# The value product of a hybrid layer in five items of 512 columns, its weights loaded in two halves of the contraction

## The chip, the core and the metric

The kernel runs on one core of one Trainium2 chip. The core has five engines with a queue each: TensorE (PE, with its weight loads as PEld), VectorE (DVE), ScalarE (ACT), GpSimd (POOL) and SyncE (SP, which here only issues DMAs). They meet at semaphores. The metric is the device time of one execution in microseconds; it is given as the median of a few runs. Data is in fp32; a product is split in a high and a rest part of the reduced type fp32r and done in three matmuls (high by high, high by rest, rest by high).

## What is computed

One layer with three token mixers and a mixture of experts for 512 prompt tokens and 64 sample tokens (576 in all, D_MODEL = 1024). Only the first step matters here: the norm, and the columns 1024 to 1535 of one wide projection, which are the values v of the attention.

```python
def token_mixers(u, lp, past):
    B, T, _ = u.shape
    proj = u @ lp['w_in']                       # w_in: 1024 x 4104
    q, k, v, xb, gb, zc, xbc, dtr = jnp.split(proj, IN_SPLITS, axis=-1)
...
    u = rmsnorm(h, lp['g_mix'])
    # v: (576, 512) = u (576, 1024) @ w_in[:, 1024:1536]
```

All else (keys, queries, convolutions, scan, gates, output, routing, experts) follows behind and is the same in both kernels.

## The kernel before, in words

**Tiles.** The 576 rows are five row tiles t = 0 to 4 (128 rows, the last 64). Each goes through four steps. `x_norm(t)`: ACT squares and sums the tile in `x0`, DVE and ACT make the inverse root, DVE scales the tile. `x_turn(t)`: TensorE transposes it in eight steps into PSUM (`za` or `zb`), DVE multiplies by the gain `gains_mix` into `u_rest`. `u_split(t)`: ACT copies it to `u_high_r` (fp32r), DVE subtracts to `u_rest_r`. The gain itself is loaded by ACT's queue, turned by TensorE (`gain_turn`) and copied by ACT (`gain_up`).

**Value weights.** w_in[:, 1024:1536] has 1024 rows (the contraction, eight blocks k of 128) by 512 columns: 2 MB in `v_raw`. SP loads it behind row tiles 0 and 1 as two halves of 256 columns, all k, in runs of 1 KB (L651), ahead of row tiles 2 to 4. `v_split(j)`, j = 0 to 3, takes one column half and four k: ACT copies to `v_high` (L1320), DVE subtracts to `v_rest` (L1725). Semaphores `high_r` and `rest_r` count these and the later splits.

**Items.** `ITEMS` lists the projection's pieces in order. Item n takes a PSUM bank of `pj` and is evicted by ACT (for v: L1363, into `v_sb`). TensorE's item n waits until item n-2 is evicted. The value product is items 0 to 9: (column half 0, tiles 0 and 1), (half 1, tiles 0 and 1), then for tiles 2, 3 and 4 half 0 and half 1. An item is 8 k by three matmuls (L791 to L793) with 256 moving columns. Behind them come the items of the keys (288 columns, two per weight unit), and so on.

**Jobs.** What has to be done ahead of item n stands in `JOBS[n]`, and each engine goes through the same list: the jobs of n in the order in which they were added, then item n. The splits of weight units were added first: unit u is split `AHEAD` = 3 items before its first use. Then x_turn(t), u_split(t) and x_norm(t+1) for t = 2, 3, 4. Steps before item 0 are written out at the end of each engine's program. The key units 1 and 2 are loaded into `first`, whose place is free from the start; SP issues the loads of the following units into the ring, where the value weights lie, when the last value item is done (L684). GpSimd writes masks and issues small parameter DMAs; it waits for the second half of the value weights, then issues the load of `w_dt` (L2391) and five parameter rows (L2395), which the step `params` ahead of the first key item needs.

Of the kernel before, what the change touches and what calls it, by code (L numbers as in the profile page):

```python
# [27 lines left out]
P = 128  # L28
# [78 lines left out]
ITEMS = [("v", c, t, 0, 0) for ts in ((0, 1), (2,), (3,), (4,)) for c in range(2) for t in ts]  # L107
# [35 lines left out]
NVP = 4  # L143
FIRST_SLOT = 2 * NSLOT
# [51 lines left out]
for _t in range(2, NT):  # L196
    job(2 * _t - 1, "x_turn", _t)
    job(2 * _t - 1, "u_split", _t)
    if _t + 1 < NT:
        job(2 * _t - 1, "x_norm", _t + 1)  # L200
job(2 * NT, "params", 0)
# [82 lines left out]
def trunk_and_experts(nc, a, o):  # L284

    ctx = ExitStack()
    with ctx:
# [293 lines left out]
        def last_bank(k):  # L581
# [6 lines left out]
            route_ps route_in routed mix_high mix_rest vp_in consts gmix_in ut_u ut_h high_r rest_r wdt_r  # L588
# [51 lines left out]
        def _(sp):  # L640
# [5 lines left out]
            for t, (o0, n) in enumerate(TT):  # L646
                src = a["x_prompt"][0, o0:o0 + n, :] if t < NT - 1 else a["x_sample"][0]
                sp.dma_start(x0[0:n, t, :], src).then_inc(x_in[t], 16)
                if t == 1:
                    for c in range(2):  # L650
                        sp.dma_start(v_raw[:, :, 256 * c:256 * (c + 1)],  # L651
                                     a["w_in"][0, :, 1024 + 256 * c:1280 + 256 * c].rearrange("(k p) n -> p k n", p=P)
                                     ).then_inc(unit_in[3 * c], 16)
# [109 lines left out]
        def _(pe):  # L763
# [31 lines left out]
            def item(n):  # L795
# [8 lines left out]
                if u in SPLIT_NO:  # L804

                    pe.wait_ge(S["rest_r"], SPLIT_NO[u + 1 if kind in "zo" else u] + 1)
                elif u is not None and kind != "v":
                    pe.wait_ge(unit_in[s], 16 * ARRIVAL[u])
# [24 lines left out]
                elif kind == "v":  # L833
                    o0, rows_n = TT[hh]
                    half = slice(256 * c, 256 * (c + 1))
                    for k in range(KD):
                        if hh == 0 and k % 4 == 0:
                            pe.wait_ge(S["rest_r"], 2 * c + k // 4 + 1)
                        uh, ur = (x[:, k, o0:o0 + rows_n] for x in (u_high_r, u_rest_r))
                        m = product(bank[0:rows_n, 0:256], (uh, ur), (v_high[:, k, half], v_rest[:, k, half]), k)  # L840
# [101 lines left out]
            def att_values(u):  # L942
                kind, hp, kb = ATT[u]
                w = att_a[u % 2]
                if u == 0:
                    wait_drained(pe, IDX[("v", 1, NT - 1)])
# [301 lines left out]
            def over_tables():  # L1248

                pe.wait_ge(S["route_in"], NT + 4)  # L1250
                for q, cols in enumerate((over_col, over_weight)):
                    for c in range(2 * NT):
# [6 lines left out]
                                             state_out, ffn_turn, logits, ranks, table, weights, params, x_turn)}  # L1259
            x_turn(0)  # L1260
            gain_turn()
# [35 lines left out]
        def _(act):  # L1297
# [53 lines left out]
            def item(n):  # L1351
# [9 lines left out]
                elif kind == "v":  # L1361
                    r = TT[hh][1]
                    m = act.activation(v_sb[0:r, hh, 256 * c:256 * (c + 1)], bank[0:r, 0:256], ACT.Copy)  # L1363
# [42 lines left out]
                if n == IDX[("v", 1, NT - 1)]:  # L1406
# [277 lines left out]
        def _(dve):  # L1684
# [37 lines left out]
            def v_split(j):  # L1722
                ks, half = slice(4 * (j % 2), 4 * (j % 2) + 4), slice(256 * (j // 2), 256 * (j // 2) + 256)
                dve.wait_ge(S["high_r"], j + 1)
                dve.tensor_tensor(v_rest[:, ks, half], v_raw[:, ks, half], v_high[:, ks, half], ALU.subtract  # L1725
# [579 lines left out]
            x_turn(0)  # L2305
            u_split(0)
            v_split(0)
            x_turn(1)
            v_split(1)
            u_split(1)  # L2310
            v_split(2)
            v_split(3)
            x_norm(2)
# [35 lines left out]
        def _(pool):  # L2349
# [39 lines left out]

            pool.wait_ge(unit_in[3], 16)  # L2390
# [228 lines left out]
```

## Time and profile before

| | |
|---|---|
| runs | 1221.39, 1208.87, 1216.23 us; median 1216.23 |
| profiled execution | span 1216.1 us |
| busy | PE 1119.0 us (92%), DVE 531.6 (44%), ACT 381.9 (31%), POOL 214.3 (18%) |
| chain that ended last | PE 56%, DMA 27%, DVE 8%, ACT 5% |

The span is the time from the first to the last instruction of one execution; busy time is the sum of an engine's instructions in it. The chain that ended last is followed back from the last instruction to what released it. The two slices that concern the change are the first ones of the 40 (30.4 us each), in which PE is busy for 4 and 9 tenths.

### The profile page before, as it was taken

To read this page: it belongs to the slowest core of one execution; us is meant where nothing else is said; L and a number is where in the kernel's file an instruction comes from. 1 tells how busy PE (TensorE), PEld (TensorE's weight loads), DVE (VectorE), ACT (ScalarE), POOL (GpSimd) and SP (SyncE) were. 2 spreads that over 40 slices of the span, in tenths; PEclk is the share of its full clock that TensorE was granted. 3 is DMA by queue.
4 is the path that set the end of the run, shared out by engine and by line. 5 is a ranking of instruction groups with operands and counts; after the bars stand their busy time and mean duration, and the time that the engine had idled before them with its cause. 6 is when DMAs were issued, how large, how long until landed. Compare 5 with 4: busy or idle time off the path is not lost.

```text
span 1216.1 us, 17158 instructions
## 1 busy us (share of the span) xinstructions
PE 1119.0 (92%) x6833; PEld 799.3 (66%) x6833; DVE 531.6 (44%) x992; ACT 381.9 (31%) x601; POOL 214.3 (18%) x230
## 2 busy tenths in 40 slices
PE   4999989899999999999999869999999999999994
PEld 4899877677988899999999853344333434333332
DVE  4331667764246465543534641333332323333336
ACT  3313666667556444433421101111110101111103
POOL 4000321332413346542310010000000000000000
PEclk9999999999999999999999959999999999999998
DMA  9279643463322212225362199999999999999982
GB/s 180 76 130 112 46 51 38 53 51 39 61 66 70 69 54 71 61 82 152 87 216 106 70 366 413 398 413 429 427 427 428 427 428 427 428 428 426 427 343 79
DMA packets 94316, 263.16 MB, mean 216 GB/s; under 512 B 5020, under 2 KB 75896, under 8 KB 81960
## 3 DMA queue, kind: packets, MB, share of 16 engines
q1 hardware_dynamic: 87664, 250.36, 61.2%
q0 software_dynamic: 3456, 6.58, 1.5%
q10 hardware_dynamic: 3128, 5.29, 1.2%
q8 instruction: 46, 0.75, 0.3%
q14 instruction: 22, 0.18, 0.0%
HBM read 258.24 MB, written 7.64 MB: 219 GB/s over the span
## 4 chain that ended last, share of the span: by engine, by line
PE 56%; DMA 27%; DVE 8%; ACT 5%; issue 3%; SPq 1%; ACTq 0%; DVEq 0%; POOLq 0%
DMA arena<-in_w_expert_up 22%; PE za L1164 12%; PE pj L791 10%; PE pj L793 9%; PE pj L792 9%; DMA ring<-in_w_in 3%; PE pj L818 2%; PE zb L1178 2%; DVE arena L1891 1%; DVE arena L1852 1%; DVE arena L1853 1%; DVE ring_r L1731 1%; PE zb L928 1%; ACT arena L1442 1%; ACT arena L1438 1%
## 5 line engine op out<-in xcount | busy, mean ns | idle before, releaser
L1164 PE MATMUL za<-arena 128*64 128x512 f32 x1024 | 231.9, 606 | 25.8 <-DMA arena<-in_w_expert_up 24.0
L791 PE MATMUL pj<-u_high_r,ring_r 128*128 128x288 f32 x736 | 224.1, 304 | 0.4 <-ACT arena L1360 0.4
L792 PE MATMUL pj<-u_rest_r,ring_r 128*128 128x288 f32 x736 | 216.7, 294 | 0.0
L793 PE MATMUL pj<-u_high_r,ring_r 128*128 128x288 f32 x736 | 216.7, 294 | 0.0
L1164 PEld LDWEIGHTS za<-arena 128*64 128x64 f32 x1024 | 73.1, 139 | 175.8 <-issue 138.6
L791 PEld LDWEIGHTS pj<-u_high_r,ring_r 128*128 128x128 f32 x736 | 138.2, 188 | 14.1 <-issue 11.6
L792 PEld LDWEIGHTS pj<-u_rest_r,ring_r 128*128 128x128 f32 x736 | 138.2, 188 | 0.6
L793 PEld LDWEIGHTS pj<-u_high_r,ring_r 128*128 128x128 f32 x736 | 138.0, 188 | 0.0
L1731 DVE TENSOR_TENSOR ring_r<-ring,ring_r 128x1024 fp32r<-128x1024 f32 x62 | 77.7, 1258 | 105.9 <-ACT ring_r L1325 105.9
L1178 PE MATMUL zb<-arena 128*64 128x512 f32 x512 | 113.6, 595 | 3.9 <-DMA arena<-in_w_expert_down 1.5
L1178 PEld LDWEIGHTS zb<-arena 128*64 128x64 f32 x512 | 36.2, 137 | 74.3 <-issue 71.5
L1325 ACT ACTIVATE ring_r<-ring 128x1024 fp32r<-128x1024 f32 x62 | 64.6, 1051 | 21.6 <-DMA ring<-in_w_in 16.7
L2570 POOL COPY arena<-arena 128x1 int32 (+1 forms) x15 | 2.7, 182 | 380.2 <-PE ms L1156 380.2
L2269 DVE SCALAR_TENSOR_TENSOR y_rest<-zb,arena,y_high 128x512 fp32r<-128x512 f32 x32 | 24.0, 751 | 89.0 <-ACT y_high L1607 89.0
L2253 DVE SCALAR_TENSOR_TENSOR arena<-arena,za 128x512 f32<-128x512 f32 x16 | 11.0, 687 | 117.9 <-PE za L1164 117.9
L1607 ACT ACTIVATE y_high<-zb,arena 128x512 fp32r<-128x512 f32 x32 | 22.0, 687 | 127.5 <-PE zb L1178 127.5
L791 PE MATMUL pj<-ring_r,u_high_r 128*128 128x256 f32 (+1 forms) x160 | 48.3, 302 | 12.5 <-ACT arena L1363 6.2
L1404 ACT ACTIVATE arena<-pj,arena 128x288 f32<-128x288 f32 x48 | 24.0, 500 | 106.4 <-PE pj L793 106.3
L2225 DVE TENSOR_TENSOR arena<-arena,pj 128x512 f32<-128x512 f32 (+1 forms) x90 | 57.2, 674 | 0.0
L1588 ACT ACTIVATE arena<-oa 128x512 f32<-128x512 f32 x16 | 9.6, 600 | 149.2 <-PE ms L1156 149.2
L2247 DVE SCALAR_TENSOR_TENSOR arena<-arena,za 128x512 f32<-128x512 f32 x16 | 11.0, 688 | 101.6 <-ACT arena L1591 101.6
L1591 ACT ACTIVATE arena<-za 128x512 f32<-128x512 f32 x16 | 9.6, 598 | 146.1 <-PE za L1164 146.1
(451 smaller groups left out, 2127.7 us busy)
## 6 DMA issues: line engine op xcount, KB each, us to landing
arena<-in_w_expert_gate SPq DMA_DIRECT2D x32, 2048.0 KB, 25.5
arena<-in_w_expert_up SPq DMA_DIRECT2D x32, 2048.0 KB, 17.7
arena<-in_w_expert_down SPq DMA_DIRECT2D x32, 2048.0 KB, 16.8
ring<-in_w_in SPq DMA_DIRECT2D x26, 512.0 KB, 8.7
ring<-in_w_gate SPq DMA_DIRECT2D x24, 512.0 KB, 4.3
arena<-in_x_prompt SPq DMA_DIRECT2D x8, 512.0 KB, 9.2
ring<-in_w_branch_out SPq DMA_DIRECT2D x8, 512.0 KB, 3.4
ring<-in_w_in SPq DMA_DIRECT2D x2, 1024.0 KB, 16.0
```

Source lines behind the costliest of these rows:

```text
L791: pe.matmul(out, left[0], right[0], start=k == 0, stop=False)
L792: pe.matmul(out, left[0], right[1], start=False, stop=False)
L793: return pe.matmul(out, left[1], right[0], start=False, stop=k == last - 1)
L818: m = pe.matmul(bank[:, 0:HALF], ring4[s][:, k, m_cols], oAT[:, k, cols], start=k == 0, stop=k == WT - 1)
L1164: m = pe.matmul(za[j * BLK:(j + 1) * BLK, b, :], xT[spare][:, k, j * BLK:(j + 1) * BLK], w[:, j * KD + k, :], start=k == 0, stop=k == KD - 1)
L1178: m = pe.matmul(zb[j * BLK:(j + 1) * BLK, q, :], hidT[:, k, j * BLK:(j + 1) * BLK], w[:, j * (DE // P) + k, q * 512:(q + 1) * 512], start= ...
L1325: act.activation(high_r[s], raw[s], ACT.Copy).then_inc(S["high_r"], 1)
L1404: m = act.activation(gsb[k % 2], bank[:, 0:HALF], ACT.Tanh, scale=0.5, bias=cpar[:, j:j + 1])
L1607: act.activation(y_high[:, half], zb[:, q, :], ACT.Copy, scale=weight_now).then_inc(S["yh_r"], 1)
L1731: dve.tensor_tensor(rest_r[s], raw[s], high_r[s], ALU.subtract).then_inc(S["rest_r"], 1)
L2225: dve.tensor_tensor(v, v, add_bank(k)[0:n, :], ALU.add).then_inc(S["sc_r"], 1)
L2269: dve.scalar_tensor_tensor(out=y_rest[:, half], in0=zb[:, q, :], scalar=weight_now, in1=y_high[:, half], op0=ALU.mult, op1=ALU.subtract).t ...
```

## The change

```diff
-ITEMS = [("v", c, t, 0, 0) for ts in ((0, 1), (2,), (3,), (4,)) for c in range(2) for t in ts]
+ITEMS = [("v", 0, t, 0, 0) for t in range(NT)]
...
+NVD = 2
...
 for _t in range(2, NT):
-    job(2 * _t - 1, "x_turn", _t)
-    job(2 * _t - 1, "u_split", _t)
+    job(_t - 1, "x_turn", _t)
+    job(_t - 1, "u_split", _t)
     if _t + 1 < NT:
-        job(2 * _t - 1, "x_norm", _t + 1)
-job(2 * NT, "params", 0)
+        job(_t - 1, "x_norm", _t + 1)
+job(NT, "params", 0)
...
# SyncE
                     for c in range(2):
-                        sp.dma_start(v_raw[:, :, 256 * c:256 * (c + 1)],
-                                     a["w_in"][0, :, 1024 + 256 * c:1280 + 256 * c].rearrange("(k p) n -> p k n", p=P)
+                        sp.dma_start(v_raw[:, 4 * c:4 * c + 4, :],
+                                     a["w_in"][0, 512 * c:512 * (c + 1), 1024:1536].rearrange("(k p) n -> p k n", p=P)
                                      ).then_inc(unit_in[3 * c], 16)
...
# TensorE, item of kind v
-                    half = slice(256 * c, 256 * (c + 1))
                     for k in range(KD):
-                        if hh == 0 and k % 4 == 0:
-                            pe.wait_ge(S["rest_r"], 2 * c + k // 4 + 1)
+                        if hh == 0 and k % 2 == 0:
+                            j = k // 2
+                            pe.wait_ge(*((S["rest_r"], j + 1) if j < NVD else (S["v_rest_p"], j - NVD + 1)))
                         uh, ur = (x[:, k, o0:o0 + rows_n] for x in (u_high_r, u_rest_r))
-                        m = product(bank[0:rows_n, 0:256], (uh, ur), (v_high[:, k, half], v_rest[:, k, half]), k)
+                        m = product(bank[0:rows_n, :], (uh, ur), (v_high[:, k, :], v_rest[:, k, :]), k)
...
+            pe.wait_ge(S["consts"], 1)
+            gain_turn()
             x_turn(0)
-            gain_turn()
             x_turn(1)
...
# ScalarE (and DVE likewise, with the subtraction)
             def v_split(j):
-                ks, half = slice(4 * (j % 2), 4 * (j % 2) + 4), slice(256 * (j // 2), 256 * (j // 2) + 256)
+                ks = slice(2 * j, 2 * j + 2)
                 act.wait_ge(unit_in[3 * (j // 2)], 16)
-                act.activation(v_high[:, ks, half], v_raw[:, ks, half], ACT.Copy).then_inc(S["high_r"], 1)
+                act.activation(v_high[:, ks, :], v_raw[:, ks, :], ACT.Copy).then_inc(S["high_r"], 1)
...
+            gain_up()
             x_norm(0)
             x_norm(1)
-            gain_up()
+            v_split(0)
             u_split(0)
-            v_split(0)
             v_split(1)
-            u_split(1)
             v_split(2)
             v_split(3)
             x_norm(2)
+            u_split(1)
...
# GpSimd
+            for j in range(NVD, NVP):
+                ks = slice(2 * j, 2 * j + 2)
+                pool.wait_ge(S["high_r"], j + 1)
+                pool.tensor_tensor(v_rest[:, ks, :], v_raw[:, ks, :], v_high[:, ks, :], ALU.subtract
+                                   ).then_inc(S["v_rest_p"], 1)
             pool.wait_ge(unit_in[3], 16)
```

In words: the value product becomes five items, one per row tile, with 512 moving columns. Its weights come as rows 0 to 511 and rows 512 to 1023, each in runs of 2 KB. The four splits take two k each, of all columns; ACT still makes all four high parts, DVE the rest parts of chunks 0 and 1, GpSimd those of chunks 2 and 3. TensorE waits for the chunks one by one in item 0 alone. The evictions of v are 512 wide. The waits of later items for `rest_r` are two lower, since DVE makes two fewer value splits. The gain's turn and copy come first. The jobs of the row tiles move with the items: x_turn(t) stands ahead of item t-1; before, it stood ahead of item 2t-1, the second half item of the tile before.

VectorE, from its turn of row tile 0 on, before (L1710 is the turn, L1719 the rest of u, L1725 the rest of a value chunk, L1696 to L1700 the norm):

```order
L1710 TENSOR_TENSOR u_rest<-za,gains_mix 128x4x128 x2
L1719 TENSOR_TENSOR u_rest_r<-u_rest,u_high_r 128x8x128
L1725 TENSOR_TENSOR ring_r<-ring,ring_r 128x4x256
L1710 TENSOR_TENSOR u_rest<-zb,gains_mix 128x4x128 x2
L1725 TENSOR_TENSOR ring_r<-ring,ring_r 128x4x256
L1719 TENSOR_TENSOR u_rest_r<-u_rest,u_high_r 128x8x128
L1725 TENSOR_TENSOR ring_r<-ring,ring_r 128x4x256 x2
L1696 TENSOR_SCALAR arena<-arena 128x1
L1699 RECIPROCAL arena<-arena 128x1
L1700 TENSOR_SCALAR arena<-arena 128x1024
L1710 TENSOR_TENSOR u_rest<-za,gains_mix 128x4x128 x2
L1719 TENSOR_TENSOR u_rest_r<-u_rest,u_high_r 128x8x128
```

and after (the same functions, two lines further down):

```order
L1712 TENSOR_TENSOR u_rest<-za,gains_mix 128x4x128 x2
L1727 TENSOR_TENSOR ring_r<-ring,ring_r 128x1024
L1721 TENSOR_TENSOR u_rest_r<-u_rest,u_high_r 128x8x128
L1727 TENSOR_TENSOR ring_r<-ring,ring_r 128x1024
L1712 TENSOR_TENSOR u_rest<-zb,gains_mix 128x4x128 x2
L1698 TENSOR_SCALAR arena<-arena 128x1
L1701 RECIPROCAL arena<-arena 128x1
L1702 TENSOR_SCALAR arena<-arena 128x1024
L1721 TENSOR_TENSOR u_rest_r<-u_rest,u_high_r 128x8x128
L1712 TENSOR_TENSOR u_rest<-za,gains_mix 128x4x128 x2
L1721 TENSOR_TENSOR u_rest_r<-u_rest,u_high_r 128x8x128
L1698 TENSOR_SCALAR arena<-arena 128x1
```

The two later value splits are gone from DVE, the first one stands ahead of the rest of u, and the norm of tile 2 ahead of the rest of u of tile 1.

VectorE a little further on, before, from the norm of tile 4 (64 rows) to the split of the second key unit (L1731):

```order
L1710 TENSOR_TENSOR u_rest<-zb,gains_mix 128x4x128 x2
L1719 TENSOR_TENSOR u_rest_r<-u_rest,u_high_r 128x8x128
L1696 TENSOR_SCALAR arena<-arena 64x1
L1699 RECIPROCAL arena<-arena 64x1
L1700 TENSOR_SCALAR arena<-arena 64x1024
L1731 TENSOR_TENSOR first_r<-first,first_r 128x1024
L1710 TENSOR_TENSOR u_rest<-za,gains_mix 128x4x64 x2
L1719 TENSOR_TENSOR u_rest_r<-u_rest,u_high_r 128x8x64
L1731 TENSOR_TENSOR first_r<-first,first_r 128x1024
```

and after, from the norm of tile 3:

```order
L1698 TENSOR_SCALAR arena<-arena 128x1
L1701 RECIPROCAL arena<-arena 128x1
L1702 TENSOR_SCALAR arena<-arena 128x1024
L1733 TENSOR_TENSOR first_r<-first,first_r 128x1024
L1712 TENSOR_TENSOR u_rest<-zb,gains_mix 128x4x128 x2
L1721 TENSOR_TENSOR u_rest_r<-u_rest,u_high_r 128x8x128
L1698 TENSOR_SCALAR arena<-arena 64x1
L1701 RECIPROCAL arena<-arena 64x1
L1702 TENSOR_SCALAR arena<-arena 64x1024
L1712 TENSOR_TENSOR u_rest<-za,gains_mix 128x4x64 x2
L1721 TENSOR_TENSOR u_rest_r<-u_rest,u_high_r 128x8x64
L1733 TENSOR_TENSOR first_r<-first,first_r 128x1024
```

The split of the first key unit, which stood behind the norm of tile 4, now stands ahead of the turn of tile 3 (`zb`), its split and that norm. ACT has the same order.

GpSimd, before, behind its masks:

```order
L2383 MEMSET arena 128x584
L2384 MEMSET arena 128x584
L2387 IOTA arena 128x32
L2388 IOTA arena 128x5
L2391 DMA arena<-in_w_in 128x8x8
L2395 DMA arena<-in_ssm_dt_bias 128x8
L2395 DMA arena<-in_ssm_a_log 128x8
L2395 DMA arena<-in_ssm_d 128x8
```

and after:

```order
L2383 MEMSET arena 128x584
L2384 MEMSET arena 128x584
L2387 IOTA arena 128x32
L2388 IOTA arena 128x5
L2393 TENSOR_TENSOR ring_r<-ring,ring_r 128x1024 x2
L2396 DMA arena<-in_w_in 128x8x8
L2400 DMA arena<-in_ssm_dt_bias 128x8
L2400 DMA arena<-in_ssm_a_log 128x8
L2400 DMA arena<-in_ssm_d 128x8
```

Two passes over value chunks now stand ahead of the load of `w_dt` and the parameter rows.

## Rows read from the trace of the kernel before

**Rows 1.** Windows by stage: stretch, length, busy us (count) of each engine, granted clock, DMA share, GB/s.

```profile
0.00:60.50 60.50, 40.73 (x287) 38.90 (x288) 23.46 (x36) 21.91 (x39) 15.40 (x36) 0.94 0.57 129
...
60.00:70.00 10.00, 10.00 (x78) 10.00 (x77) 2.68 (x9) 1.96 (x6) 0.00 (x0) 1.00 0.90 204
...
725.00:1216.00 491.00, 446.15 (x2040) 184.54 (x2036) 169.80 (x294) 59.57 (x106) 17.83 (x29) 0.98 0.94 397
```

**Rows 2.** TensorE's waits, 0 to 320 us: total us, times, longest.

```profile
PE pj L791 <- ACT arena L1363: 6.2, 1, 6.2
...
PE pj L791 <- DVE u_rest_r L1719: 3.0, 3, 1.1
```

**Rows 3.** Time line of TensorE: start us, us, what [idle before <-releaser].

```profile
14.60 0.55 PE L791 MATMUL pj<-ring_r,u_high_r 128*128 128x256 f32 x1 [3.34 <-DVE ring_r L1725]
...
18.79 0.28 PE L792 MATMUL pj<-ring_r,u_high_r 128*128 128x256 f32 x1
...
28.59 0.58 PE L791 MATMUL pj<-ring_r,u_high_r 128*128 128x256 f32 x1 [6.17 <-ACT arena L1363]
...
29.18 0.42 PE L793 MATMUL pj<-ring_r,u_rest_r 128*128 128x256 f32 x1
...
29.40 0.41 PE L791 MATMUL pj<-ring_r,u_high_r 128*128 128x256 f32 x1
...
38.11 0.36 PE L791 MATMUL pj<-ring_r,u_high_r 128*128 128x256 f32 x1 [0.95 <-DVE u_rest_r L1719]
...
41.06 1.03 PE L785 MATMUL zb<-arena 128*128 128x128 f32 x8
```

**Rows 4.** SP's time line, times to landing of the v and x loads, DMA queue q10.

```profile
59.82 10.63 SPq L684 DMA_DIRECT2D ring<-in_w_in  x4
...
L651 SPq DMA_DIRECT2D ring<-in_w_in x2: 582/660/737, 1.7 to 2.5; - x2
DMA to landing us min/median/max: 10.0/16.0/22.0
...
DMA to landing us min/median/max: 3.7/20.2/23.1
...
q10 hardware_dynamic: 15, 0.00, 11.2%
```

**Rows 5.** Windows of the first loads, the cache tiles, and the clock's fall.

```profile
2.40:5.80 3.40, 0.00 (x0) 0.00 (x0) 0.10 (x1) 1.70 (x4) 3.24 (x6) 1.00 0.96 331
5.80:11.70 5.90, 4.04 (x17) 3.31 (x17) 3.33 (x8) 2.32 (x6) 5.82 (x15) 1.00 1.06 225
11.70:24.50 12.80, 7.81 (x48) 7.64 (x48) 5.91 (x6) 3.31 (x4) 0.94 (x4) 1.00 0.91 151
...
25.00:26.00 1.00, 0.00 (x0) 0.00 (x0) 0.40 (x1) 1.00 (x2) 1.00 (x2) 0.80 1.15 234
...
35.00:39.00 4.00, 3.04 (x25) 2.87 (x25) 2.57 (x6) 2.58 (x5) 0.00 (x0) 1.00 1.02 383
```

**Rows 6.** Time line of ScalarE.

```profile
24.51 2.00 ACT L1320 ACTIVATE ring_r<-ring 128x1024 fp32r<-128x1024 f32 x2 [7.77 <-DMA ring<-in_w_in]
...
41.26 0.38 ACT L1363 ACTIVATE arena<-pj 128x256 f32<-128x256 f32 x1 [2.72 <-PE pj L793]
43.45 1.06 ACT L1315 ACTIVATE u_high_r<-u_rest 128x1024 fp32r<-128x1024 f32 x1 [1.81 <-DVE u_rest L1710]
```

**Rows 7.** Time line of VectorE.

```profile
42.13 1.29 DVE L1710 TENSOR_TENSOR u_rest<-zb,gains_mix 128x512 f32<-128x512 f32 x2 [2.88 <-PE zb L785]
44.54 1.23 DVE L1719 TENSOR_TENSOR u_rest_r<-u_rest,u_high_r 128x1024 fp32r<-128x1024 f32 x1 [1.12 <-ACT u_high_r L1315]
...
46.28 0.74 DVE L1700 TENSOR_SCALAR arena<-arena 64x1024 f32<-64x1024 f32 x1
```

**Rows 8.** Groups by line and form: GpSimd.

```profile
L2486 POOL TENSOR_TENSOR arena<-arena 128x1024 f32<-128x1024 f32 x4 | 9.6, 2395 | 18.1 <-DVE arena L1951 18.1
```

**Rows 9.** Time line of TensorE, expert stage.

```profile
799.78 3.60 PE L1164 MATMUL za<-arena 128*64 128x512 f32 x16
```

More of the change, by code:

```diff
@@ L587, in trunk_and_experts @@
         names = """
-            route_ps route_in routed mix_high mix_rest vp_in consts gmix_in ut_u ut_h high_r rest_r wdt_r
+            route_ps route_in routed mix_high mix_rest vp_in consts gmix_in ut_u ut_h high_r rest_r v_rest_p wdt_r
             gb_zero par_in bc_in kp_in par_up ssq_r var_r std_r xn_r pe_par xt_ps ut_r pj_full pj_act pj_dve
@@ L804, in item @@
                 if u in SPLIT_NO:
-                    pe.wait_ge(S["rest_r"], SPLIT_NO[u + 1 if kind in "zo" else u] + 1)
+                    pe.wait_ge(S["rest_r"], SPLIT_NO[u + 1 if kind in "zo" else u] + 1 - NVD)
                 elif u is not None and kind != "v":
@@ L945, in att_values @@
                 if u == 0:
-                    wait_drained(pe, IDX[("v", 1, NT - 1)])
+                    wait_drained(pe, IDX[("v", 0, NT - 1)])
                     pe.wait_ge(S["vp_in"], 16)
@@ L1362, in item @@
                     r = TT[hh][1]
-                    m = act.activation(v_sb[0:r, hh, 256 * c:256 * (c + 1)], bank[0:r, 0:256], ACT.Copy)
+                    m = act.activation(v_sb[0:r, hh, :], bank[0:r, :], ACT.Copy)
                 elif kind == "z":
@@ L1405, in item @@
                 m.then_inc(S["pj_act"], 1)
-                if n == IDX[("v", 1, NT - 1)]:
+                if n == IDX[("v", 0, NT - 1)]:
                     act.wait_ge(*drained(n))
@@ L1722, in v_split @@
             def v_split(j):
-                ks, half = slice(4 * (j % 2), 4 * (j % 2) + 4), slice(256 * (j // 2), 256 * (j // 2) + 256)
+                ks = slice(2 * j, 2 * j + 2)
                 dve.wait_ge(S["high_r"], j + 1)
-                dve.tensor_tensor(v_rest[:, ks, half], v_raw[:, ks, half], v_high[:, ks, half], ALU.subtract
+                dve.tensor_tensor(v_rest[:, ks, :], v_raw[:, ks, :], v_high[:, ks, :], ALU.subtract
                                   ).then_inc(S["rest_r"], 1)
@@ L2305, in _ @@
             x_turn(0)
+            v_split(0)
             u_split(0)
-            v_split(0)
+            v_split(1)
             x_turn(1)
-            v_split(1)
+            x_norm(2)
             u_split(1)
-            v_split(2)
-            v_split(3)
-            x_norm(2)
             for n in range(NITEM + 1):
@@ L2388, in _ @@
             pool.iota(tok_id, [[P, NT]], base=0, channel_multiplier=1).then_inc(S["ids_r"], 1)
+            for j in range(NVD, NVP):
+                ks = slice(2 * j, 2 * j + 2)
+                pool.wait_ge(S["high_r"], j + 1)
+                pool.tensor_tensor(v_rest[:, ks, :], v_raw[:, ks, :], v_high[:, ks, :], ALU.subtract
+                                   ).then_inc(S["v_rest_p"], 1)
             pool.wait_ge(unit_in[3], 16)
```

## Prediction, made before the changed kernel ran

> **What bounds the kernel now.** Read first the windows by stage [rows 1]: up to 60.5 us TensorE is busy for 40.7 us, from 725 us on the DMA engines are busy 0.94 of the time with the expert weights. All edits lie before 60 us. From 60 to 70 us TensorE has no gap. Nothing behind that point has a time of its own: the loads of the ring are released by the last value item, the experts by the mixers, so I let a microsecond won or lost before 60 us pass whole to the end.
>
> Then TensorE's waits [rows 2]: in the value product it waits 6.2 us once and 3.0 us in three pieces. The time line of its instructions [rows 3] shows where. It starts at 14.60; up to 18.79 it starts 19 matmuls of 256 columns, one every 0.22 us, and from there every 0.12 us, so the fast pace comes 4.2 us after the start. After two items (column half 0, tiles 0 and 1) it stops at 22.4 and goes on at 28.59, at the slow pace again (29.18 to 29.40 is 0.22). The granted clock averages 0.80 from 25 to 26 us [rows 5]: 1.00 is 2.4 GHz, 0.50 is 1.2 GHz, so it fell at 25.6 or so, after TensorE had stood idle for over 3 us, and the stall costs more than its length. The release is put down to the ACT eviction, but ScalarE itself had been waiting: the row at 24.51 [rows 6] waited 7.8 us for the second half of the weights. It was issued at about 2.5 and took 22.0 us to land, the first half 10.0 [rows 4]. So a late load, not arithmetic, is the largest loss; after it come three waits of about 1 us, one per row tile (the row at 38.11 is one).
>
> **The DMA side** [rows 5]: 225 GB/s from 5.8 to 11.7 us, then only 151 GB/s up to 24.5, both with the engines busy for nearly all of it. From 35 to 39 us the cache tiles, whose runs are 2 KB, move at 383 GB/s. The value weights have runs of 1 KB, and their successors will have 2 KB.
>
> **What the change moves, step by step.**
>
> *Landing of the weights.* The first half (rows 0 to 511, all 512 columns) lands at L0, the second at L1. Bounds of L1: the first two x tiles, 1 MB, have moved by about 5.8 us (3.4 us at 331 GB/s, [rows 5]); at the cache tiles' pace the 2 MB then take 5.5 us, so 11.3 us, and about 12.5 with a microsecond for the POOL parameters that share the engines; at the pace of today 24.5. The value weights jump rows of the w_in matrix, which the cache tiles do not, so I do not take the first. If what one run loses stays as it is and only the number of runs halves, today's 18.7 us (5.8 to 24.5) fall to somewhat over half, about 10 us. I take L1 = 16.0 and L0 = 10.0 (today 11.7).
>
> *Start.* The gain's DMA, alone on its queue (q10), moves 15 packets between 1.5 and 1.9 us [rows 4], so gain_up ahead of x_norm(0) costs ScalarE nothing: x tile 0, issued at 0.82, is there 3.7 us later, at 4.5. DVE no longer waits for the gain; what takes its place is L0. From L0: ACT split 1.0 (two take 2.00 in the row at 24.51), DVE split 1.23 and DVE's rest of u 1.23 (1024 elements each, as in the row at 44.54, [rows 7]): ready at L0 + 3.5 = 13.5, 1.1 us earlier than 14.60.
>
> *Item 0.* 24 matmuls of 512 columns. The expert products have that width: 16 of them in 3.60 us with the last one's tail [rows 9], about 0.22 us each, so an item takes 5.3 us, against 2.95 us (38.11 to 41.06, [rows 3]) for one of 256. Five cost 26.5, ten cost 29.5: 3 us less. At the slow clock one of them takes 0.43. From 13.5: twelve matmuls need chunks 0 and 1 and are done at 18.1 (nine slow ones, three fast). Chunk 2: ACT at 16.0 to 17.05, then POOL. A POOL pass of 128x1024 with two inputs is at 2.4 us [rows 8], twice that of DVE; 2.4 is taken, 2.0 to 3.0 are the bounds. Ready at 19.45; chunk 3 behind it on POOL, 21.85. TensorE waits 1.35 us, runs six, waits 1.05 us, runs six: item 0 ends at 23.3, that is L1 + 7.3. I count no fall of the clock for waits that short: the waits of 1 us today leave the next item at 2.95 us. On ScalarE and DVE nobody waits for POOL; queued behind its splits are the DMAs of w_dt and five parameter rows, wanted at item 5, over 15 us later.
>
> *Items 1 to 4.* After an item ends (41.24), today's rows give the turn of the next tile on TensorE 0.9, DVE 42.13 to 43.42, ACT to 44.51, DVE to 45.77 [rows 6, 7]: u ready 4.5 us after the end, and the following norm ready at 47.02, 5.8 us after. Item 1 (turn of 0.9, then 5.3) ends 6.2 us after item 0, so neither the next turn nor item 2 waits: the three waits of 1 us are gone. But the split of the first key unit now falls into the job list ahead of item 2, **in front of** turn and split of tile 3: 1.0 us on ACT and 1.2 on DVE are ahead of them, with an eviction of twice the width (0.6 against 0.38). The norm of tile 4 is then ready 7.7 us after item 1's end, and TensorE, which wants it at 6.2, waits 1.5 us: a new wait. From item 1's end: 6.2 + 1.5 + 0.6 (turn of 64 rows, two thirds of 0.9 as an estimate) + 2 x 5.3 = 18.9. The last item ends 6.2 + 18.9 = 25.1 us after item 0.
>
> *Sum.* End of the value product = L1 + 7.3 + 25.1 = L1 + 32.4; today it is 59.8, where SP issues the next ring load [rows 4]. The change is L1 - 27.4: with L1 = 16.0, **-11.4 us**. The profiled execution has 1216.1 us (its span), the median of the three runs is 1216.23, so it stands for them: 1216.2 - 11.4 = 1204.8 us. Behind the last item all relations stay: the four items of the two key units in `first` cover the landing of the first ring unit today (no gap from 60 to 70), and as much after.
>
> A rule weighs against this: the Trainium skill, DMA: Bandwidth & Descriptors, "Why small descriptors are slow", gives a packet a fixed overhead of about 3 cycles beside one cycle per 32 bytes; going from 1 KB to 2 KB it would save some 4% (an estimate from that page). The 383 GB/s of the cache tiles against 151 do not fit an overhead that small, unless the place in HBM and not the run matters. By the rule the sum would end at rival 2 below.
>
> **Rivals.** (1) *The load stops mattering.* L1 at or under 13: the new chunks are always ready, item 0 runs from 13.0 (DVE's queue sets that: its turn of x tile 0, then three passes) to 20.3 at the two clocks, the end is 45.4: -14.4 us, 1201.8. For it: the 383 GB/s; against: the strided rows. (2) *The bytes count, not the runs.* L1 stays 24.5 as now. Item 0 does twelve matmuls, waits until 27.9, comes back at the slow clock and ends at 32.7; the end is 57.8: -2.0 us, 1214.2. Even then the short waits and the 3 us of columns are won, and the clock's loss stays. For it: the engines were busy during the 151 GB/s, so they stalled inside packets, and a stall may go by bytes. (3) *Slower.* Today the first column half lets two items through before the second half is there; after the change no item can end before both row halves are in. If the second half comes later than 27.4 us, the kernel is slower; at 30 it loses 2.6 us (1218.8), and to lose 1% it would have to come after 39.6 us. What could do it: the `first` loads (runs of 512 bytes), which queue behind the value loads, may now be issued earlier, with half the value packets ahead of them, and share the engines. Against: they stand behind in the queue.
>
> A lesser point: the Trainium skill, GPSIMD Engine Reference, says that GpSimd shares its SBUF interfaces with VectorE when that runs two SBUF inputs. The pass of 2.4 us in the trace [rows 8] is twice DVE's time; if the split were 3.0 us instead of 2.4, item 0 would end 1.2 us later. This moves the sum little, and I leave it in the range.
>
> **How the numbers follow.** Forecast (L1 from 13.5 to 20): 0.52, its own range -14 to -7, 1202 to 1209. Rival 1: 0.20. Rival 2 (L1 from 20 to 27): 0.24. Rival 3: 0.04. Range: from rival 1 less 4 us for the scatter of a few runs (before: 1208.87 to 1221.39) to rival 2: 1198 to 1214. Over 1% faster means more than 12.2 us, about what a measurement of this kernel can tell from no change: L1 under 15.2. That is rival 1 and two fifths of the forecast, 0.41. Slower by 1% 0.02; within 1% 0.57.
>
> **What would show it.** In the profile after: L1 in the row of the value load's landing; ACT's first row of chunk 2 released by that DMA; two POOL rows of about 2.4 us in a chain; TensorE's first 512-column matmul near 13.5 and the gap in the middle of item 0 under 3 us with no fall of the clock; no wait for u_rest_r ahead of item 2, one of about 1.5 us for the norm ahead of the last turn; the last value item near 48 us. I am wrong if L1 lies above 20 or under 13, if POOL needs much over 3 us a chunk, if the 1.5 us wait is absent, or if the time won by 48 us is lost again at the first ring unit or behind it.

## The result

| | before | changed |
|---|---|---|
| median of 13 runs | 1213.11 us (1208.87 to 1221.39) | 1208.78 us (1201.34 to 1212.78) |
| ratio of the two | | 0.9949, 95% interval 0.9931 to 0.9967 |
| span of the profiled execution | 1216.1 us | 1206.4 us |
| last value item ended | 59.8 us | 53.6 us |

The change makes the kernel half a percent faster, 6.2 us by the ratio and 4.3 us by the medians; forecast were 11.4. Run again beside the last experiments, the changed kernel gave 0.9941 (0.9919 to 0.9963). The two spans differ by 9.7 us, more than the medians: single executions of one kernel scatter by several us behind the changed part, so below each experiment is judged first by when its last value item ends, which is when SP issues the next ring load.

TensorE's waits after the change, against [rows 2] (us in total, times, longest):

```profile
PE za L786 <- DVE arena L1702: 5.2, 2, 3.8
PE pj L792 <- DVE u_rest_r L1721: 3.4, 1, 3.4
...
PE pj L792 <- POOL ring_r L2393: 3.1, 1, 3.1
...
PE pj L792 <- DVE arena L1772: 0.6, 1, 0.6
```

The wait of 6.2 us for the second half of the weights and the three waits for `u_rest_r` are gone (the 3.4 us are the start of item 0, 3.3 before). New are 3.1 us for POOL, 1.4 us of the 5.2 us for L1702 (the norm ahead of the last turn; the rest is before x tile 0), and 0.6 us at the keys. The time line of TensorE, against [rows 3]:

```profile
14.15 0.79 PE L792 MATMUL pj<-ring_r,u_high_r 128*128 128x512 f32 x1 [3.36 <-DVE u_rest_r L1721]
...
18.30 0.39 PE L794 MATMUL pj<-ring_r,u_rest_r 128*128 128x512 f32 x1
...
21.79 0.80 PE L792 MATMUL pj<-ring_r,u_high_r 128*128 128x512 f32 x1 [3.10 <-POOL ring_r L2393]
...
22.81 0.63 PE L794 MATMUL pj<-ring_r,u_rest_r 128*128 128x512 f32 x1
23.24 0.63 PE L792 MATMUL pj<-ring_r,u_high_r 128*128 128x512 f32 x1
...
27.08 1.35 PE L786 MATMUL za<-arena 128*128 128x128 f32 x8
...
33.75 1.04 PE L786 MATMUL zb<-arena 128*128 128x128 f32 x8
...
41.62 0.71 PE L786 MATMUL za<-arena 64*128 64x64 f32 x8 [1.38 <-DVE arena L1702]
...
64.61 0.40 PE L792 MATMUL pj<-u_high_r,first_r 128*128 128x288 f32 x1 [0.64 <-DVE arena L1772]
```

Item 0 starts at 14.15, its first twelve matmuls are issued by 18.30, then nothing until 21.79. Behind the gap two starts lie 0.43 us apart (22.81 to 23.24), the price at 1.2 GHz. Item 0 ends at 27.3. Loads and helpers, against [rows 4], [rows 6], [rows 7] and [rows 8]: first the value loads' line, us to landing:

```profile
DMA to landing us min/median/max: 8.9/12.4/16.0
```

Then the time lines of SP, ScalarE, GpSimd and VectorE:

```profile
53.57 10.74 SPq L685 DMA_DIRECT2D ring<-in_w_in  x4
...
10.64 1.06 ACT L1322 ACTIVATE ring_r<-ring 128x1024 fp32r<-128x1024 f32 x1 [3.15 <-DMA ring<-in_w_in]
...
18.25 2.00 ACT L1322 ACTIVATE ring_r<-ring 128x1024 fp32r<-128x1024 f32 x2 [4.66 <-DMA ring<-in_w_in]
...
34.45 1.05 ACT L1327 ACTIVATE first_r<-first 128x1024 fp32r<-128x1024 f32 x1
...
53.58 0.59 ACT L1365 ACTIVATE arena<-pj 64x512 f32<-64x512 f32 x1 [3.98 <-PE pj L794]
...
19.39 4.68 POOL L2393 TENSOR_TENSOR ring_r<-ring,ring_r 128x1024 fp32r<-128x1024 f32 x2 [6.62 <-ACT ring_r L1322]
...
21.95 2.67 DVE L1702 TENSOR_SCALAR arena<-arena 128x1024 f32<-128x1024 f32 x1
...
35.53 1.23 DVE L1733 TENSOR_TENSOR first_r<-first,first_r 128x1024 fp32r<-128x1024 f32 x1 [2.14 <-ACT first_r L1327]
36.67 1.28 DVE L1712 TENSOR_TENSOR u_rest<-zb,gains_mix 128x512 f32<-128x512 f32 x2
39.08 1.23 DVE L1721 TENSOR_TENSOR u_rest_r<-u_rest,u_high_r 128x1024 fp32r<-128x1024 f32 x1 [1.12 <-ACT u_high_r L1317]
```

The second half lands at 18.2 us (24.5 before), the first at 10.6. The DMAs and the granted clock in windows, against [rows 5]:

```profile
5.80:11.70 5.90, 3.63 (x16) 3.28 (x16) 3.28 (x7) 2.50 (x6) 5.83 (x15) 1.00 1.05 197
11.70:18.20 6.50, 4.05 (x11) 3.26 (x12) 4.70 (x5) 1.89 (x2) 0.88 (x4) 0.74 1.00 212
...
20.00:21.00 1.00, 0.00 (x0) 0.00 (x0) 0.00 (x0) 1.00 (x2) 1.00 (x1) 0.94 1.11 208
21.00:22.00 1.00, 0.21 (x1) 0.21 (x2) 0.37 (x3) 0.78 (x4) 1.00 (x2) 0.50 1.14 150
...
26.00:27.00 1.00, 1.00 (x4) 0.69 (x3) 0.00 (x0) 0.00 (x0) 1.00 (x3) 0.50 0.95 52
...
28.00:29.00 1.00, 1.00 (x8) 0.87 (x7) 0.54 (x1) 0.00 (x0) 0.00 (x0) 1.00 0.49 13
```

The column behind POOL's is the granted clock: 0.94 from 20 to 21 us, 0.50 from 21 on, 1.00 again from 28. An average of 0.94 over that microsecond puts the fall at 20.9, when TensorE had been idle for some 2.2 us (since 18.69).

### The profile page after: what moved, and what is told of

The parts are those of the page before. It is cut to its first block, busy times and chain, and to the rows that moved or that the text cites. A ratio compares the mean times of both kernels' runs of the same rounds, so it can differ in the third digit from the quotient of the medians.

```text
span 1206.4 us, 16909 instructions
## 1 busy us (share of the span) xinstructions
PE 1118.0 (93%) x6713; PEld 791.8 (66%) x6713; DVE 532.0 (44%) x990; ACT 380.9 (32%) x596; POOL 219.0 (18%) x232
## 4 chain that ended last, share of the span: by engine, by line
PE 58%; DMA 25%; DVE 9%; ACT 5%; issue 2%; SPq 0%; POOL 0%; DVEq 0%; POOLq 0%
DMA arena<-in_w_expert_up 22%; PE za L1165 12%; PE pj L792 10%; PE pj L793 10%; PE pj L794 10%; PE pj L819 2%; PE zb L1179 2%; DMA ring<-in_w_in 2%; DVE arena L1893 1%; DVE arena L1854 1%; DVE ring_r L1733 1%; DVE arena L1855 1%; PE zb L929 1%; DVE arena L1868 1%; PE ms L1092 1%
## 5 line engine op out<-in xcount | busy, mean ns | idle before, releaser
L1165 PE MATMUL za<-arena 128*64 128x512 f32 x1024 | 233.7, 610 | 23.6 <-DMA arena<-in_w_expert_up 21.7
L792 PEld LDWEIGHTS pj<-u_high_r,ring_r 128*128 128x128 f32 x736 | 138.1, 188 | 12.6 <-issue 11.1
L2536 POOL TENSOR_TENSOR merged<-merged,arena 128x288 f32<-128x288 f32 x32 | 35.1, 1096 | 81.1 <-DVE arena L1785 80.9
## 6 DMA issues: line engine op xcount, KB each, us to landing
arena<-in_w_expert_up SPq DMA_DIRECT2D x32, 2048.0 KB, 17.9
ring<-in_w_in SPq DMA_DIRECT2D x2, 1024.0 KB, 12.4
```

Of the source, the lines that this page charges most:

```text
L792: pe.matmul(out, left[0], right[0], start=k == 0, stop=False)
L1165: m = pe.matmul(za[j * BLK:(j + 1) * BLK, b, :], xT[spare][:, k, j * BLK:(j + 1) * BLK], w[:, j * KD + k, :], start=k == 0, stop=k == KD - 1)
L2536: pool.tensor_tensor(v, v, gtmp[k % 2], ALU.add).then_inc(S["gm_r"], 1)
```

## Experiments

All are edits to the changed kernel. "End" is the time at which SP issues the ring load behind the last value item, 53.6 us in the changed kernel; "landing" is that of the second half of the value weights, 18.2.

### GpSimd out of the value splits

```diff
-NVD = 2
+NVD = 4
...
             x_turn(1)
+            v_split(2)
+            v_split(3)
             x_norm(2)
```

(On VectorE; with it the loop on GpSimd is empty and the later waits for `rest_r` count all four.)

> Edit to the changed kernel: DVE makes the rest parts of all four value chunks, GpSimd none. In the changed kernel the second half landed at 18.25 us, POOL had chunk 2 ready at 21.75 (2.36 us a pass), TensorE stood idle from 18.7 to 21.79, and the granted clock fell at 21.1 us, so that the twelve matmuls of 0.43 us behind it cost 2.4 us more than at 0.23. Theory A (the missing 3 us of the forecast are the clock, brought down by the POOL wait): with DVE's 1.22 us a chunk the wait is 1.9 us, chunk 2 ready at 20.55, chunk 3 at 21.7, item 0 ends at 23.1 if the clock holds, and the last value item at 49.3 instead of 53.57, near 4.2 us earlier; the norm pass of DVE that took 2.67 us beside POOL is back at 0.75. Theory B (the clock falls for any wait here, long or short): same landing, the clock low for the same stretch, item 0 ends at 25.7, the last item at 51.9. Both scale with the landing of the second half, which I expect within 1 us of 18.25.

Measured: ratio to before 0.9928 (0.9899 to 0.9957). The time lines of SP, VectorE and TensorE:

```profile
49.43 21.75 SPq L685 DMA_DIRECT2D ring<-in_w_in  x5
...
19.11 2.36 DVE L1727 TENSOR_TENSOR ring_r<-ring,ring_r 128x1024 fp32r<-128x1024 f32 x2 [1.57 <-ACT ring_r L1322]
...
22.01 0.75 DVE L1702 TENSOR_SCALAR arena<-arena 128x1024 f32<-128x1024 f32 x1
...
19.86 0.40 PE L794 MATMUL pj<-ring_r,u_rest_r 128*128 128x512 f32 x1
20.39 0.50 PE L792 MATMUL pj<-ring_r,u_high_r 128*128 128x512 f32 x1
```

The last item ends at 49.4, as theory A said. DVE has both chunks ready by 21.5. TensorE is hardly held: from 19.86 to 20.39 is 0.53 us, 0.3 us more than the pace of 0.23, and the idle time between the two rows is 0.13 us. The next matmuls follow after 0.34 and then some 0.23 us: the clock held. But the wait of 1.9 us that theory A counted with did not occur. Item 0 began late in this run, at 15.27, because the first half landed later (11.76 instead of 10.64), and stayed at the slow pace up to 19.27, so TensorE wanted chunk 2 only at 20.3. The forecast end came out, by way of a shorter wait than was forecast, and the 4.1 us cannot be split between VectorE's pace and the clock from this run. DVE's norm pass of 1024 elements is at 0.75 us again, against 2.67 at 21.95 beside POOL.

### TensorE kept busy through the wait

```diff
                         if hh == 0 and k % 2 == 0:
                             j = k // 2
+                            if k == 4:
+                                for _ in range(12):
+                                    pe.matmul(oa[:, :], v_high[:, 0, 0:P], v_high[:, 0, :], start=True, stop=True)
```

> Edit to the changed kernel: twelve extra matmuls of 512 columns into an unused PSUM bank ahead of TensorE's wait for chunk 2 in item 0; their result is used nowhere. POOL and the loads stay. Theory A (the clock is the missing term): TensorE is busy through the wait, the granted clock stays at 1.00 from 21 to 28 us, chunk 2's six matmuls take 1.4 us, TensorE waits 0.9 us for chunk 3, item 0 ends at 25.5 instead of 27.3, the last value item at 51.5 instead of 53.6, about 2 us earlier, although more work is done. Rival (the slow matmuls there are not the clock but the competition with POOL, DVE or the DMAs for the memory): they stay at 0.43 us and the extra ones only delay; last item at 53.6 or later.

Measured: ratio to before 0.9942 (0.9918 to 0.9966). The time lines of TensorE and SP:

```profile
22.26 0.39 PE L792 MATMUL pj<-ring_r,u_high_r 128*128 128x512 f32 x1
...
24.03 0.50 PE L792 MATMUL pj<-ring_r,u_high_r 128*128 128x512 f32 x1 [0.25 <-POOL ring_r L2396]
...
51.71 21.92 SPq L685 DMA_DIRECT2D ring<-in_w_in  x5
```

A window of it, the granted clock behind POOL's column:

```profile
22.00:23.00 1.00, 1.00 (x6) 0.81 (x5) 1.00 (x1) 0.48 (x1) 1.00 (x1) 1.00 1.19 208
```

Landing, POOL and all loads are as before (POOL 19.20 to 23.97), but the clock stays at 1.00, the six matmuls of chunk 2 run at 0.23 us, and the last item ends at 51.7, 1.9 us earlier although twelve matmuls were added. So the slow matmuls behind the gap are the clock's, not a competition for the memory, and keeping the clock is worth 1.9 us at that place against this profile of the changed kernel. Against its second profile (below), which waited 2.38 us and had its clock back sooner, it is worth 0.6 us. The ratios do not tell the two kernels apart (0.9942 and 0.9949).

### The key unit's split behind the row tiles' jobs

```diff
-for _u in SPLITS:
-    job(SPLIT_AT[_u], "split", _u)
 for _t in range(2, NT):
...
         job(_t - 1, "x_norm", _t + 1)
+for _u in SPLITS:
+    job(SPLIT_AT[_u], "split", _u)
```

> Edit to the changed kernel: the splits of weight units are added to the job lists behind the row tiles' jobs, so the first key unit is split behind turn, split and norm. Theory (the new wait ahead of the last turn, 1.38 us, comes from that split): the wait is gone, the last value item ends 1.4 us earlier after the end of item 1 (18.2 instead of 19.6 us), and the first key item still finds its weights. Rival (the norm chain itself is that long): it stays, since norm of tile 4 would be ready at 5.8 us and be wanted at 6.6.

Measured in one execution (1209.47 us, so the time says nothing at this size). The last turn, and SP:

```profile
39.30 0.71 PE L786 MATMUL za<-arena 64*128 64x64 f32 x8
...
51.25 21.82 SPq L685 DMA_DIRECT2D ring<-in_w_in  x5
```

The turn at 39.30 has no wait any more (1.38 us in the changed kernel). Item 1 ended at 33.1 and the last at 51.25: 18.2 us, as expected, against 19.6. The other 0.9 us of the earlier end lies ahead of item 1's end. There the clock came back sooner: the turn behind item 0 starts at 26.49 here and takes 1.04 us, against 27.08 and 1.35.

### Runs of 1 KB, and rows that lie side by side

```diff
# e4_runs_1k
-                        sp.dma_start(v_raw[:, 4 * c:4 * c + 4, :],
-                                     a["w_in"][0, 512 * c:512 * (c + 1), 1024:1536].rearrange("(k p) n -> p k n", p=P)
-                                     ).then_inc(unit_in[3 * c], 16)
+                        for q in range(2):
+                            sp.dma_start(v_raw[:, 4 * c:4 * c + 4, 256 * q:256 * (q + 1)],
+                                         a["w_in"][0, 512 * c:512 * (c + 1), 1024 + 256 * q:1280 + 256 * q]
+                                         .rearrange("(k p) n -> p k n", p=P)).then_inc(v_in[c], 16)
# (the waits for the two halves follow: each counts its two DMAs)
# e7_contiguous
-                                     a["w_in"][0, 512 * c:512 * (c + 1), 1024:1536].rearrange("(k p) n -> p k n", p=P)
+                                     a["w_expert_gate"][0, 0, 512 * c:512 * (c + 1), :].rearrange("(k p) n -> p k n", p=P)
```

> Edit to the changed kernel: each row half of the value weights is loaded by two DMAs of 256 columns, so in runs of 1 KB as before, in the order of the rows as after. Theory A (the run length brought the second half from 24.5 to 18.25 us): it lands near 24 us again, chunk 2 is ready near 27.6, the last value item ends near 59. Rival (the bytes and their order decide, the run length does not): it lands within 1 us of 18.25 and the last item ends near 53.6.

> Edit to the changed kernel: the value weights are read from the first expert's gate matrix, 1024 rows of 2 KB that lie side by side in HBM, instead of columns of w_in, whose rows are 16.4 KB apart. Same sizes, same targets, same 2 KB runs; the value projection is computed with the wrong weights, which changes which experts the tokens go to, so only the first 60 us are read. Theory A (the place in HBM costs, not the packets): the second half lands near 12.5 us, as at the cache tiles' 383 GB/s. Theory B (engines, order or the small DMAs cost): it lands near 18 us as before.

Measured with 1 KB: ScalarE gets the second half at 21.75, SP is at the next ring load at 56.06:

```profile
21.75 2.00 ACT L1324 ACTIVATE ring_r<-ring 128x1024 fp32r<-128x1024 f32 x2 [4.88 <-DMA ring<-in_w_in]
...
56.06 9.87 SPq L687 DMA_DIRECT2D ring<-in_w_in  x4
```

Measured with the rows side by side: the value loads' line with the time to landing (the second half was issued at 2.2):

```profile
DMA to landing us min/median/max: 8.2/9.3/10.4
```

A window of the same run:

```profile
5.80:11.70 5.90, 3.65 (x16) 3.27 (x16) 4.03 (x9) 3.22 (x6) 5.83 (x14) 1.00 1.02 358
```

And the time lines of GpSimd and VectorE, beside each other:

```profile
13.90 5.72 POOL L2393 TENSOR_TENSOR ring_r<-ring,ring_r 128x1024 fp32r<-128x1024 f32 x2
...
17.32 3.39 DVE L1721 TENSOR_TENSOR u_rest_r<-u_rest,u_high_r 128x1024 fp32r<-128x1024 f32 x1
```

Neither theory of the first was right. With runs of 1 KB the second half lands at 21.7 (24.5 before, 18.2 after the change). That splits the 6.3 us into 3.5 for the run length and 2.8 for the rest, first of all the order (row halves instead of column halves). The split is from one profile each, and the run with 1 KB also issues four DMAs for two, over 3.0 us instead of 1.0, which was not tried apart. With rows side by side it lands at 12.6 us, at 358 GB/s from 5.8 to 11.7 us where the changed kernel has 197: theory A. The DMA engines were busy in both (share 1.02 and 1.05). The same 2 KB runs at the same place in the queue cost 5.6 us more when they are cut out of rows of 16.4 KB. So what slows the value load is where it lies in HBM. The run changes the matrix together with the distance of its rows; that the distance is the cause is likely and not shown. Why the longer runs soften it was not tried further.

### The neighbours of the value load

```diff
# e5_first_late, SyncE
                 if u == 0:
                     continue
+                if u == 1:
+                    sp.wait_ge(unit_in[3], 16)
# e6_params_late, GpSimd: the loop over PAR_ROWS and the two state loads
# stand behind the value splits instead of ahead of the masks
```

> Edit to the changed kernel: SP waits for the second half of the value weights before it issues the two `first` loads (issued from 4.6 us on in the changed kernel). Theory A (rival 3 of the prediction in part: these 512-byte runs share the engines with the value load and delay it): the second half lands clearly before 18.0 us, by 1 to 3 us. Theory B (each engine takes its packets in the order of issue, what stands behind does not matter): it lands at 18.0 to 18.7 as in four runs so far.

> Edit to the changed kernel: GpSimd issues its twelve small parameter DMAs only after its value splits, at about 24 us. Theory A (the small software-queued packets slow the value load in its second part, 151 GB/s before the change): the second half lands by 15 to 16 us, the last value item near 50. Theory B (they carry 0.1 MB and do not matter): 18.0 to 18.7 us again.

The time line of ScalarE with the `first` loads late:

```profile
18.25 2.00 ACT L1324 ACTIVATE ring_r<-ring 128x1024 fp32r<-128x1024 f32 x2 [4.62 <-DMA ring<-in_w_in]
```

The same with the parameter DMAs late:

```profile
17.81 2.00 ACT L1322 ACTIVATE ring_r<-ring 128x1024 fp32r<-128x1024 f32 x2 [4.09 <-DMA ring<-in_w_in]
```

The landing is 18.2 and 17.8 us, against 17.9 to 18.6 in the eight other profiles with these value loads. Neither the `first` loads nor the small DMAs are what slows it: both landings are those of theory B; that each engine takes its packets in the order of issue, the reason it gave, is not shown by them. The `first` loads land later when held back (SP goes on at 29.1 instead of 27.0) and nobody waits. The ends are 52.6 and 51.3 us, earlier than 53.6, but not by the load: TensorE came to its wait for chunk 2 later (at 19.5 and 19.7 instead of 18.7), because the slow pace at its start lasted longer, and waited 2.30 and 1.69 us. With the second of these the clock held.

### Two matmuls of 256 columns for one of 512

```diff
-                        m = product(bank[0:rows_n, :], (uh, ur), (v_high[:, k, :], v_rest[:, k, :]), k)
+                        for q in range(2):
+                            half = slice(256 * q, 256 * q + 256)
+                            # the three matmuls of product() on bank[0:rows_n, half] with v_high and v_rest [:, k, half]
```

> Edit to the changed kernel: each matmul of 512 columns of the value product is made as two of 256 into the same PSUM bank; everything else stays. It prices the wide items: the last four items take 5.53 us each in the changed kernel, and two half items took 2 x 2.95 = 5.9 us before. Theory: 5.8 to 5.9 us each, so the width is worth 0.3 to 0.4 us an item, 1.5 to 2 us in all, less than the 3 us forecast. Rival (the forecast's size): 6.1 us each.

From the turn ahead of item 1 to the one ahead of item 2 it is 6.62 us here and 6.37 in the run with TensorE kept busy, whose clock held as well (25.52 and 31.89 there):

```profile
25.52 1.03 PE L786 MATMUL za<-arena 128*128 128x128 f32 x8
...
32.14 1.03 PE L786 MATMUL zb<-arena 128*128 128x128 f32 x8
...
46.69 0.60 ACT L1373 ACTIVATE arena<-pj 128x512 f32<-128x512 f32 x1 [4.53 <-PE pj L849]
...
52.15 0.59 ACT L1373 ACTIVATE arena<-pj 64x512 f32<-64x512 f32 x1 [3.91 <-PE pj L849]
```

So the width is worth 0.25 us for a tile of 128 rows, and for the last tile, of 64 rows, nothing (5.46 us between the last two evictions, 5.53 from 48.05 to 53.58 in the changed kernel). That is 1.0 us in all if item 0 gains as much, below the 3 us forecast and below this experiment's own theory too.

### Both mends together

```diff
# e9_dve_late = e1_dve_all + e3_key_split_late
# e11_dve_late_warm = e9_dve_late + six extra matmuls ahead of k == 4
# e10_after_again = the changed kernel, unchanged
```

> The changed kernel with both mends: DVE makes all four rest parts, and the key splits stand behind the row tiles' jobs. If the two effects add (they sit in different places, one in item 0, one ahead of item 3), the last value item ends near 48.0 us (49.4 with DVE alone, less 1.4), 5.5 us ahead of the changed kernel's 53.6 and 11.8 ahead of the kernel before; ratio to before near 0.990. Rival: taking POOL out moves the work of two chunks in front of DVE's norm of tile 2, and with the second mend that chain becomes the bound: last item at 49.4 or later. What is won at the last value item should show whole in the time; if not, the later stages give it back.

> The changed kernel once more, beside the others on the same chip, for the scatter of its landing and of its clock. Expected: second half at 18.0 to 18.7 us, last value item at 51.5 (clock held) to 53.6 (clock down in item 0), ratio to before 0.995.

> The kernel with both mends and six extra matmuls of 512 columns ahead of TensorE's wait for chunk 2. If the shorter wait of the mended kernel (1.9 us when item 0 starts at 14.2) still brings the clock down at times, this one is as fast or faster by up to 2 us at the last value item; if the clock holds there anyway, both end within 0.3 us of each other, near 48.0.

Measured against before: 0.9919 (0.9899 to 0.9939), 0.9941 (0.9919 to 0.9963) and 0.9918 (0.9890 to 0.9946). The intervals of all three overlap with each other and with that of the changed kernel. In the first TensorE waits 0.41 us for chunk 2 and not at all ahead of the last turn, but 0.97 us at the keys:

```profile
20.30 0.50 PE L792 MATMUL pj<-ring_r,u_high_r 128*128 128x512 f32 x1 [0.41 <-DVE ring_r L1727]
...
23.16 1.04 PE L786 MATMUL za<-arena 128*128 128x128 f32 x8
...
35.93 0.71 PE L786 MATMUL za<-arena 64*128 64x64 f32 x8
...
59.26 0.40 PE L792 MATMUL pj<-u_high_r,first_r 128*128 128x288 f32 x1 [0.97 <-DVE arena L1772]
...
47.88 22.49 SPq L685 DMA_DIRECT2D ring<-in_w_in  x5
```

TensorE's wait in item 0 of the repeated changed kernel, and its SP:

```profile
21.73 0.66 PE L792 MATMUL pj<-ring_r,u_high_r 128*128 128x512 f32 x1 [2.38 <-POOL ring_r L2393]
...
52.33 10.79 SPq L685 DMA_DIRECT2D ring<-in_w_in  x4
```

Both effects add: the last item ends at 47.9 us (expected 48.0), 5.7 us ahead of the changed kernel and 4.4 ahead of its repetition. The extra matmuls then bring nothing (48.1): the clock holds anyway, behind a wait of 0.41 us, since here too item 0 began late (14.81) and slowly; the wait of 1.9 us was not met. The repeated changed kernel ended at 52.3, with its clock back earlier (turn behind item 0 at 26.17 instead of 27.08). In the time, the mends give 0.9919 against 0.9941 and 0.9949, some 3 us where the last value item is 4.4 to 5.7 us earlier. The intervals overlap, so that the version with both mends is the faster one is likely, not shown. The medians are 1204.65 us with both mends, 1206.24 for the changed kernel beside it and 1214.76 before.

Where the rest of the 4.4 to 5.7 us went can be read from the traces. The stretch from the last value item to the first reload of an x tile is 559.7 us before, 558.8 and 559.7 in the two profiles of the changed kernel, 563.0 with both mends and 557.6 with the six extra matmuls on top. So these profiles show no fixed loss there: that stretch scatters, and it scatters with the clock. Taken in windows of 10 us from 60 to 320 us (a mean of 0.90 stands for 2 us at the lower level), the granted clock adds up to 10.2 us at the lower level before, 6.8 and 10.2 in the changed kernel, 13.8 with both mends and 3.4 with the extra matmuls. Over all 13 profiles the order is the same, from 3.4 us low and a stretch of 557.4 to 17.0 us low and 564.8. The 5.4 us by which the last two differ are close to the 5.2 us that half the clock costs over 10.4 us. Why the clock fell more often in some executions was not tried.

## Why the prediction was right or wrong

Direction and range held (1198 to 1214, measured 1208.78), and so did within 1%, the likeliest of the three chances. The narrower range of the forecast itself, -14 to -7 us, did not hold, although L1 lay inside its 13.5 to 20. The size was off by nearly half: -11.4 forecast, -6.2 measured by the ratio, -4.3 by the medians. In the profile the last value item ended at 53.6 us and not at 48.4. The 5.2 us, step by step:

* **Landing of the weights** (taken L1 = 16.0, L0 = 10.0). Measured 18.2 and 10.6: 2.2 us. The bounds 12.5 and 24.5 held. The step from runs of 1 KB to 2 KB ("what one run loses stays as it is and only the number of runs halves") was half right: it is worth 3.5 us of the 6.3, and the rest came with the order of the halves, which the prediction did not price. The argument that the column cut from w_in would not reach the cache tiles' pace was right: 12.6 us side by side, 18.2 cut out. The rule of the Trainium skill, DMA: Bandwidth & Descriptors, "Why small descriptors are slow", by which the prediction estimated a saving of some 4%, fell too low. From 5.8 us on the load took 12.4 us with runs of 2 KB and 15.9 with runs of 1 KB in the same order of rows, over a fifth less; the measurement decides.
* **"I count no fall of the clock for waits that short."** This step failed, and it is the one in which the mechanism was wrong and not only a size. The wait for POOL's chunk was 3.1 us instead of 1.35, since L1 was 2.2 us later and TensorE only 0.6 us, and the clock fell within it. Twelve matmuls at 0.43 instead of 0.23 us cost 2.4 us, less the wait of 0.9 us for the last chunk that then disappears, and the turn behind them took 0.3 us more: about 2 us together. The run with TensorE kept busy gives back 1.9 us. Over nine profiles of item 0: the clock fell behind waits of 3.10, 3.08, 2.53, 2.38 and 2.30 us, and not behind 1.69, 1.55, 0.41 and 0.13. In two of the five, those of 2.53 and 2.30 us, it fell only after TensorE had come back at the fast pace, some 0.6 and 1 us later. With the L1 that was forecast the wait would have been 1.35 us and, by these nine, the step harmless. What the nine do not show is a limit: the waits differ also in when TensorE's first fast matmuls came ahead of them. The prediction took the clock from waits of 1 us alone; it should have been priced both ways.
* **Item 0 and POOL.** The term was right: POOL 2.34 us a pass (2.4 taken). That this was the path to mend was not drawn from it: DVE alone is 1.2 us a chunk and idle there, and with DVE the last item ends 4.1 us earlier (2.9 against the repeated changed kernel).
* **Items of 5.3 us.** Measured 5.53 from 48.05 to 53.58 (0.23 us a matmul, where the expert rows gave 0.22): 0.9 us over four items. The saving of 3 us over ten narrow items shrank to 1.8 by these durations (5 x 5.53 = 27.7 against 29.5), and the width alone is worth some 1.0 us by the experiment.
* **The new wait ahead of the last turn**, forecast 1.5 us behind the key unit's split, measured 1.38, and gone when the split is moved. The three waits of 1 us for `u_rest_r` are gone as said. These two were the best steps.
* **The start**: 13.5 forecast, 14.15 measured; L0 was 0.6 us later, which is all of it.
* **"Behind the last item all relations stay."** Nearly: the first ring unit took 8.3 us to land instead of 6.8, its split on DVE stood ahead of a key eviction, and TensorE waited 0.64 us at 64.61, where before it had no gap [rows 1]. In all twelve profiles of the changed kernel and its variants that unit took 7.7 to 8.6 us to land. Why it lands later is open.
* **The baseline.** The sum was put on 1216.2 us; over 13 runs the median before is 1213.11. That the three runs lay high hid part of the miss: 1204.8 forecast and 1208.78 measured are 4.0 apart, the two differences 5.2 (7.1 by the medians). That the time came so near to 1204.8 is luck to that extent.

Rival 1 (load stops mattering) needed L1 under 13, which the side-by-side run has: there no chunk is waited for in item 0, but the last item ends at 48.0 and not at the 45.4 of that rival, since the slow pace lasted to 19.2 in item 0 and the later items and the last turn cost what they cost in the changed kernel. Rival 2 did not come, rival 3 neither; its mechanism, that the `first` loads delay the second half, is refuted by holding them back.

## What to carry to other kernels

When an edit moves a wait of TensorE, price it twice, with the clock held and with the clock down: here a wait of 3.1 us cost 2 us more behind it, one of 2.4 us some 0.6 us, and one of 1.7 us nothing. Chunks that TensorE waits for in turn belong on the faster engine, even if another stands idle: with half of them on GpSimd, at 2.34 us a pass instead of 1.22, chunk 2 was ready 3.5 us after the load had landed (18.25 to 21.79) instead of 2.4 (17.93 to 20.30). And a load cut out of a wide matrix should be costed from a row of that same matrix, not from a load that lies side by side: 2 MB landed 5.6 us later. Last, when a gain of a few us does not show in the time, add up the clock of the later stages before looking for a loss there.

## What the runs showed of the hardware

* DVE's single-input pass over 1024 elements took 2.67 us when it fell into POOL's two-input passes, 0.75 us otherwise (21.95 in the changed kernel, 22.01 with DVE alone). In the side-by-side run both have two inputs: DVE 3.39 us instead of 1.23, POOL 2.86 instead of 2.34. The Trainium skill, GPSIMD Engine Reference, "Key points", says that GpSimd shares its SBUF interfaces with VectorE for instructions in a 2-port mode or with two SBUF inputs; the pass of 3.39 us agrees, and shows that DVE can pay nearly threefold. In which mode the single-input pass ran no view says.
* These passes of DVE look as if they stood still until POOL was through: they end 0.55 us (24.62 after 24.07) and 1.09 us (20.71 after 19.62) behind POOL's end, and in the seven other profiles with POOL passes in this place it is 0.54 to 0.56 us each time. That is an inference from the ends. And not every DVE pass beside POOL pays: in the side-by-side run the two-input pass at 13.39 (1.21 us) and the turn at 14.53 (1.27 us for two) lie beside POOL's record from 13.90 on and took their usual time.
* While columns of w_in (rows 16.4 KB apart) were loaded, the DMA queues moved 151 to 225 GB/s (225 and 151 before, with runs of 1 KB; 197 and 212 in the changed kernel, with 2 KB). With the same amount from rows that lie side by side it was 358 in the window from 5.8 to 11.7 us.
